# Filling tiles set around the first attention's compressed scores, a lighter first and last phase, and the second attention's maxima ahead of due evictions

## The reference

```python
# first block: compressed branch, with 31 blocks of keys and values
kc = compress(kv[0], ...); vc = compress(kv[1], ...)
pc = masked_softmax(q @ kc.T, cmp_end <= t)
o_c = pc @ vc
...            # selected and window branches: causal softmax over 512 keys
o = gates[0] * o_c + gates[1] * o_s + gates[2] * o_w
c = silu(layernorm(causal_dwconv(c_val * sigmoid(c_gate))))   # 31 taps
h = h + (sigmoid(za) * (o @ w_o) + sigmoid(zb) * (c @ w_co + b)) @ w_out
# second module, first block: 16 heads
s = q @ k.T + c[:, None] - c[None, :]      # c: running sum of log forget gates
m = softmax(causal(s)) @ v @ w_out
```

## Time and profile before

| | us |
|---|---|
| timed executions | 2183.87, 2184.62, 2186.61 |
| profiled execution, its time | 2185.68 |
| its span | 2183.9 |
| TensorE busy | 2146.1 |
| VectorE busy | 1013.6 |
| GpSimd busy | 933.8 |
| ScalarE busy | 869.6 |

### The profile page before, as it was taken

The page is one execution under the profiler, slowest core; times in us unless marked ns, Lnnn a source line. Parts: engine busy times, 40 slices in busy tenths (PEclk is TensorE's granted clock), DMA queues, the critical chain, the costliest instruction groups (busy, mean ns, idle before and its releaser), DMA issues.

```text
span 2183.9 us, 25305 instructions
## 1 busy us (share of the span) xinstructions
PE 2146.1 (98%) x10192; PEld 1758.8 (81%) x10192; DVE 1013.6 (46%) x1637; ACT 869.6 (40%) x1358; POOL 933.8 (43%) x424
## 2 busy tenths in 40 slices
PE   9999999999999999999999999999999999999998
PEld 7877778888888887777778888888888888888886
DVE  5877775445524235666634422313653345122134
ACT  5434346444424254444434422324532244233234
POOL 5722124434444455322225444444554454444446
PEclk9999999999999999999999999999999999999999
DMA  4421112233233332211122333322223323332222
GB/s 159 148 75 41 47 49 80 94 97 106 97 97 97 97 115 78 70 57 49 49 67 88 97 97 97 97 97 87 97 87 97 97 85 99 97 97 96 97 80 85
DMA packets 53829, 193.27 MB, mean 88 GB/s; under 512 B 6096, under 2 KB 6224, under 8 KB 53712
## 3 DMA queue, kind: packets, MB, share of 16 engines
q1 hardware_dynamic: 52992, 189.81, 27.0%
q10 hardware_dynamic: 720, 1.84, 0.3%
HBM read 189.53 MB, written 2.10 MB: 88 GB/s over the span
## 4 chain that ended last, share of the span: by engine, by line
PE 89%; DVE 6%; ACT 3%; issue 1%; DMA 0%; POOL 0%; DVEq 0%; ACTq 0%; POOLq 0%
PE ps L519 27%; PE ps L521 27%; PE ps L520 27%; PE ps L733 1%; DVE ps L1209 1%; PE ps L982 1%; PE ps L713 1%; PE ps L1000 1%; PE ps L725 1%; ACT w_hi L1855 1%; PE ps L615 1%; DVE xg_lo L1169 1%; PE ps L1007 0%; DVE ps L1730 0%; PE ps L715 0%
## 5 line engine op out<-in xcount | busy, mean ns | idle before, releaser
L472 POOL TENSOR_TENSOR w_lo<-w_raw,w_hi 128x1024 fp32r<-128x1024 f32 x352 | 852.6, 2424 | 1211.4 <-ACT w_hi L1855 1211.3
L519 PE MATMUL ps<-xg_hi,w_hi 128*128 128x512 f32 x1688 | 674.1, 399 | 5.4 <-POOL w_lo L486 2.8
L521 PE MATMUL ps<-xg_hi,w_lo 128*128 128x512 f32 x1688 | 661.2, 392 | 0.0
L520 PE MATMUL ps<-xg_lo,w_hi 128*128 128x512 f32 x1688 | 660.7, 391 | 0.0
L1855 ACT ACTIVATE w_hi<-w_raw 128x1024 fp32r<-128x1024 f32 x352 | 372.3, 1058 | 626.5 <-PE ps L521 623.8
L519 PEld LDWEIGHTS ps<-xg_hi,w_hi 128*128 128x128 f32 x1688 | 318.8, 189 | 69.3 <-issue 3.0
L521 PEld LDWEIGHTS ps<-xg_hi,w_lo 128*128 128x128 f32 x1688 | 318.5, 189 | 67.9
L520 PEld LDWEIGHTS ps<-xg_lo,w_hi 128*128 128x128 f32 x1688 | 319.2, 189 | 59.4
L521 PE MATMUL ps<-h_hi,w_lo 128*128 128x512 f32 x688 | 267.8, 389 | 0.0
L519 PE MATMUL ps<-h_hi,w_hi 128*128 128x512 f32 x688 | 267.8, 389 | 0.0
L520 PE MATMUL ps<-h_lo,w_hi 128*128 128x512 f32 x688 | 267.8, 389 | 0.0
(11 more groups left out here) (342 smaller groups left out, 2462.7 us busy)
## 6 DMA issues: line engine op xcount, KB each, us to landing
w_raw<-in_weights SPq DMA_DIRECT2D x352, 512.0 KB, 3.5
out_x<-mixed SPq DMA_DIRECT2D x8, 256.0 KB, 2.1
resid<-in_x SPq DMA_DIRECT2D x3, 512.0 KB, 7.4
p_raw<-in_p ACTq DMA_DIRECT2D x3, 512.0 KB, 3.6
resid<-in_x SPq DMA_DIRECT2D x2, 256.0 KB, 4.0
last_gain<-in_last_gain SPq DMA_DIRECT2D x1, 512.0 KB, 4.6
w_raw<-in_weights SPq DMA_DIRECT2D x1, 256.0 KB, 4.0
w_raw<-in_weights ACTq DMA_DIRECT2D x1, 256.0 KB, 4.4
```

What stands on the lines that cost most here:

```text
L472: pool.tensor_tensor(w_lo[:, slot, :], w_raw[:, u % RAW, :], w_hi[:, slot, :].bitcast(F32), ALU.subtract).then_inc(w_ready, 1)
L519: pe.matmul(o, w, x, start=start, stop=False)
L520: pe.matmul(o, w, xl, start=False, stop=False)
L521: return pe.matmul(o, wl, x, start=False, stop=stop)
```

## The change

In the first attention, three triples stand before `cmp_scores(0)` and one inside it, one inside each of the three later `cmp_scores`; phase 8 has nine triples in its steps where it had sixteen (the eight after the steps stay), and phases 1 to 7 keep theirs. The low parts of the compressed keys and values are made from PSUM without copies in SBUF. Two taps more stand before the phases, and the first tap of each step of phase 0 is gone, so the last taps move to the last step of phase 7. The eviction steps shift with the table (in phases 1 to 7 from steps 0 and 2 mostly to 1 and 3). In the second attention, VectorE's and ScalarE's due evictions go behind the next maxima and exponentials, the last low part of a pair goes behind the first maxima of the next pair, and the forget row of the next pair is made by ScalarE. Six matmuls that nobody reads stand before the last part of the output projection.

```diff
-EARLY_TAPS = 62
+EARLY_TAPS = 64
-LN_ADD = ((0, 1), (4, 0), (7, 3))
-NSA_FILL = [((2, 2),) * 4] + [((2, 2),) * 4, ((2, 2, 2), (2, 1), (2, 2), (2, 1))] * 4
+LN_ADD = ((2, 2), (4, 0), (7, 3))
+NSA_FILL = [((6, 2), (2, 2), (2, 2), (2, 2))] + [((2, 2), (2, 2), (2, 2), (2, 2, 1)), ((2, 2, 2), (2, 1), (2, 2), (2, 1))] * 3 + [
+    ((2, 2), (2, 2), (2, 2), (2, 2, 0)), ((2, 1, 1), (1, 1), (1, 1), (1, 0))]
...
-            def cmp_scores(p):
+            def cmp_scores(p, between):
...
+                    if qi < QB - 1 and between[qi]:
+                        fill(between[qi])
...
+            fill(3)
             pe.wait_ge(c_act, 5)
...
-            pe.wait_ge(s_cmp["klo"], 2)
+            pe.wait_ge(s_cmp["klo"], 4)
...
-                            cmp_scores(0)
-                            fill(pieces[0])
+                            cmp_scores(0, (0, 1, 0))
+                            fill(2)
...
-                        cmp_scores(j // 2 + 1)
+                        cmp_scores(j // 2 + 1, (0, pieces[2], 0))
...
             for p in range(8):
                 fox_pair(p)
+            for _ in range(6):
+                pe.matmul(ps[:, 2, :], ident_r[:], ident_r[:].unsqueeze(1).to_broadcast([P, QB, P]), start=True, stop=True)
...
-            dve.tensor_copy(kc_f[0:HD, 0:NC1], ps[0:HD, 4, 0:NC1]).then_inc(s_cmp["out"], 1)
-            dve.tensor_copy(kc_f[HD:P, 0:NC1], ps[HD:P, 4, NC1:2 * NC1]).then_inc(s_cmp["out"], 1)
-            dve.tensor_tensor(vc_f[:], ps[0:2 * NC1, 5, 0:P], own[:], ALU.mult).then_inc(s_cmp["out"], 1)
+            dve.tensor_tensor(ps[0:2 * NC1, 5, 0:P], ps[0:2 * NC1, 5, 0:P], own[:], ALU.mult).then_inc(s_cmp["out"], 1)
...
-            low(kc_lo[:], kc_f[:], kc_hi[:], s_cmp["klo"])
-            low(vc_lo[:], vc_f[:], vc_hi[:], s_cmp["klo"])
+            for g in range(2):
+                rows = slice(g * HD, (g + 1) * HD)
+                low(kc_lo[rows, 0:NC1], ps[rows, 4, g * NC1:(g + 1) * NC1], kc_hi[rows, 0:NC1], s_cmp["klo"])
...
+            dve.tensor_tensor(vc_lo[:], ps[0:2 * NC1, 5, 0:P], vc_hi[:].bitcast(F32), ALU.subtract).then_inc(s_cmp["klo"], 2)
...
-                    if tapped[0] < CT * CONV_TAPS:
+                    if j and tapped[0] < CT * CONV_TAPS:
                         taps(1)
...
-                mx(0); nrm(0); evict(0)
-                mx(1); nrm(1)
+                mx(0)
+                if p:
+                    fox_evict(p - 1, 11)
+                    out_low(p - 1, 1)
+                nrm(0)
+                mx(1); evict(0); nrm(1)
...
-                evict(1)
-                mx(2); nrm(2); evict(2)
-                mx(3); nrm(3)
-                if p < 7:
-                    head_rows(p + 1)
+                mx(2); evict(1); nrm(2)
+                mx(3); evict(2); nrm(3)
...
-                ex(0); evict(0); ex(1)
+                ex(0); ex(1); evict(0)
...
-                evict(1); ex(2); evict(2); ex(3); evict(3)
+                ex(2); evict(1); ex(3)
+                if p < 7:
+                    act.activation(c_head[:], c_rows[:], ACT.Copy, scale=head_sel[:, p + 1:p + 2]).then_inc(A2["crow"], 1)
+                evict(2); evict(3)
```

More of the change, by code:

```diff
@@ L827, in _ @@
                     if j % 2 and i == QB - 1 and j < 7:
-                        cmp_scores(j // 2 + 1)
+                        cmp_scores(j // 2 + 1, (0, pieces[2], 0))
+                    elif j == 7 and i == QB - 1:
+                        fill(pieces[2])
                     fill(pieces[1])
@@ L1263, in _ @@
                 dve.tensor_tensor(kv_dup[HD:P, j, 0:S - 1], ps[HD:P, BANK[uu], 1:S], R[HD:P, 0, 1:S], ALU.mult).then_inc(bank_free, 1)
-            dve.memset(kc_f[:], 0.0).then_inc(s_cmp["out"], 1)
+            for t in (kc_hi, kc_lo):
+                dve.tensor_scalar(t[:, NC1:NCP], ones[:, 0:1], 0.0, None, ALU.mult).then_inc(s_cmp["out"], 1)
             dve.wait_ge(s_cmp["dup"], 4)
@@ L1305, in _ @@
             dve.wait_ge(unit_done, U["cmp_out"] + 1)
[L1306 to L1309 removed]
+            dve.tensor_tensor(ps[0:2 * NC1, 5, 0:P], ps[0:2 * NC1, 5, 0:P], own[:], ALU.mult).then_inc(s_cmp["out"], 1)
             dve.memset(token[:, 12:13], 0.0).then_inc(bank_free, 1)
             dve.wait_ge(s_cmp["khi"], 2)
[L1312 to L1314 removed]
+            for g in range(2):
+                rows = slice(g * HD, (g + 1) * HD)
+                low(kc_lo[rows, 0:NC1], ps[rows, 4, g * NC1:(g + 1) * NC1], kc_hi[rows, 0:NC1], s_cmp["klo"])
+            dve.wait_ge(s_cmp["khi"], 3)
+            dve.tensor_tensor(vc_lo[:], ps[0:2 * NC1, 5, 0:P], vc_hi[:].bitcast(F32), ALU.subtract).then_inc(s_cmp["klo"], 2)
             dve.wait_ge(s_kv["lo"], 2)
@@ L1437, in _ @@
                     nsa_evict(nsa_made(j, i - 1) if i else nsa_made(j - 1, QB - 1) if j else 0)
-                    if tapped[0] < CT * CONV_TAPS:
+                    if j and tapped[0] < CT * CONV_TAPS:
                         taps(1)
-                    if i == 1 and br == 0 and j < 8:
+                    if i == (1 if j else QB - 1) and br == 0 and j < 8:
                         cmp_normalise(p)
@@ L1648, in _ @@
             dve.wait_ge(s_fg["dve"], 6)
-            def head_rows(p):
-                dve.tensor_scalar(c_head[:], c_rows[:], head_sel[:, p:p + 1], None, ALU.mult).then_inc(A2["crow"], 1)
-            head_rows(0)
+            dve.tensor_scalar(c_head[:], c_rows[:], head_sel[:, 0:1], None, ALU.mult).then_inc(A2["crow"], 1)
             counted = [3, 3]
@@ L1682, in lo, with out_low @@
                     split_turned(A2, e0 + 4 * hd + kb, kb % 2, (fpt_hi, fpt_lo), kb)
-                def out_low(hd):
+                def out_low(p, hd):
                     rows = slice(hd * HD, (hd + 1) * HD)
@@ L1690, in evict @@
                     fox_evict(p, i)
-                mx(0); nrm(0); evict(0)
-                mx(1); nrm(1)
+                mx(0)
[4 more added lines that the diff above has]
+                mx(1); evict(0); nrm(1)
                 dve.wait_ge(A2["vhi"], p + 1)
                 low(fv_lo[:], ps[:, 4, :].rearrange("p (a b) -> p a b", b=P), fv_hi[:], A2["vlo"])
-                evict(1)
-                mx(2); nrm(2); evict(2)
-                mx(3); nrm(3)
-                if p < 7:
-                    head_rows(p + 1)
+                mx(2); evict(1); nrm(2)
+                mx(3); evict(2); nrm(3)
                 evict(3)
-                lo(0, 0); lo(0, 1); evict(4); lo(0, 2); evict(5); lo(0, 3); evict(6); lo(1, 0); out_low(0); lo(1, 1); evict(7)
-                lo(1, 2); evict(8); lo(1, 3); evict(9); evict(10); out_low(1); evict(11)
+                lo(0, 0); lo(0, 1); evict(4); lo(0, 2); evict(5); lo(0, 3); evict(6); lo(1, 0); out_low(p, 0); lo(1, 1); evict(7)
+                lo(1, 2); evict(8); lo(1, 3); evict(9); evict(10)
+                if p == 7:
+                    out_low(7, 1)
             while counted[0] < 5:
@@ L1981, in _ @@
             highs(U["cmp_out"] + 1 + RING)
-            act.wait_ge(s_cmp["out"], 4)
-            copy_hi(kc_hi[:], kc_f[:], s_cmp["khi"])
-            copy_hi(vc_hi[:], vc_f[:], s_cmp["khi"])
+            act.wait_ge(unit_done, U["cmp_out"] + 1)
+            for g in range(2):
+                rows = slice(g * HD, (g + 1) * HD)
+                copy_hi(kc_hi[rows, 0:NC1], ps[rows, 4, g * NC1:(g + 1) * NC1], s_cmp["khi"])
+            act.wait_ge(s_cmp["out"], 3)
+            copy_hi(vc_hi[:], ps[0:2 * NC1, 5, 0:P], s_cmp["khi"])
             highs(U["gates"] + 1 + RING)
```

4 lines of the change are left out of this document (removed).

## The result

The changed kernel took 2193.22 us (median of 6 runs, 2191.39 to 2195.42); the kernel before, on the same chip, 2186.05 us (6 runs, 2183.87 to 2188.07). The ratio is 1.0036, with a 95% interval of 1.0025 to 1.0046: slower by 7 to 8 us, where 2175.6 was predicted. The profiled execution took 2192.44 us, with a span of 2190.7.

What follows compares the result with a forecast made beforehand. TensorE, busy 98% of the span, was taken as the bound, losing time to waits and the 1.2 GHz clock. Terms -5.8 - 1.0 + 0.3 - 1.3 - 1.3 = -9.1 us gave 2175.6 us, range 2170.8 to 2181.3.

Steps and rivals of the forecast that it cites:

- The opening: Start of the first attention: the 4.06 us wait and 4.5 of low clock go, four triples cost 2.76: -5.8 us.
- rival B: The opening still waits, klo 2 us late and the clock low again: 4.5 us come back, 2180.1 us; chance 0.06.
- The later compressed scores: Three later compressed scores, one triple inside each: +2.07 us, two low-clock episodes go, -3.1: -1.0 us.
- Evictions of phases 1 to 7 moved: Evictions go from steps 0 and 2 to 1 and 3: 0 us, bounded by 0.3 for each of seven phases.
- Phase 8: Seven triples leave, but the dependency chain sets the length; ScalarE's queue ends 0.55 earlier, ln_sum costs +0.85: +0.3 us.
- Second attention: Evictions behind maxima and forget rows on ScalarE cut waits, with some new ones in pairs 2, 5 and 7: -1.3 us.
- Unread matmuls: Six matmuls before the output projection's last part fit a 1.41 us wait and keep the clock up: -1.3 us.
- A: The clock falls anyway: two or three low-clock episodes of 1.54 us come back, 2179.4 us; chance 0.17.
- D: Slower than before: phase 8 starved, TensorE at 1.2 GHz for all of it, costing 10.3 us: 2185.8 us; chance 0.04.

Runs made afterwards that it cites:

- run 10: The kernel before with only the opening's new low parts of compressed keys and values, made from PSUM without SBUF copies: 2177.29 us, ratio 0.9961.
- run 4: The changed kernel with the filling table, taps and normalising steps of the kernel before, and eight unread matmuls for the opening's three triples: 2175.13 us, ratio 0.9956.
- run 7: run 4 without the eight unread matmuls in the opening: 2174.85 us, ratio 0.9949.
- run 12: run 7 with the eviction of fv moved ahead of the maxima again in the last pair alone: 2173.54 us, ratio 0.9946.
- run 13: The changed kernel with GpSimd's four colliding w_lo waiting until VectorE's prob_s of the step is done, in phases 0, 2, 4 and 6: 2183.22 us, ratio 0.9998.
- run 1: The changed kernel with VectorE's normalising of the compressed scores moved off the eviction steps in phases 0, 2, 4 and 6: 2183.79 us, ratio 0.9992.
- padded: The changed kernel with 21 unread matmuls in phase 8 where the seven removed filling triples had stood: 2190.07 us, ratio 1.0022.
- run 14: run 13 with one wait more: GpSimd's w_lo of phase 7's last step waits for the last ln_sum: 2180.38 us, ratio 0.9990.
- run 3: The kernel before with the second attention's part of the change alone, without the six unread matmuls: 2184.13 us, ratio 0.9998.

## Why the prediction was wrong

- **The opening, -5.8: right.** No wait before the first compressed scores and full clock behind; the subtractions from PSUM take 0.41 us for two and 0.28 beside a running `w_lo`. The second scores of phase 0, the mark that was named, start at 132.60 instead of 138.47, 5.9 us earlier. One bound was added up wrongly: with 2 us of waiting and the low clock both back, the term would be -5.8 + 2 + 4.5 = +0.7 and not -1.3, and rival B 2182.1 and not 2180.1, above the stated range; neither came, so it changes nothing here. Not seen: the three triples were not needed. Without them and the two taps the wait is 0.21 us and the whole opening gives 8.5 (run 10).
- **The later compressed scores, -1.0: wrong in size.** The triples cost their 2.07. Of the two low stretches there the one at 268 went and the other stayed, at 168: +0.5 where -1.0 was forecast. Run 10, whose later filling is that of the kernel before, has neither in its trace, and runs 4, 7 and 12 with the same filling have one near 260 (6.8, 3.4 and 3.4 us long): these stretches were no fixed cost of this place, and the -3.1 for them was not sure to be had.
- **Evictions of phases 1 to 7 moved, 0 with a bound of 0.3 each: the step that failed.** It priced VectorE's eviction at 0.7 and `w_hi` at 1.06 us and stopped there. It did not follow `w_hi` to the engine that waits for it, GpSimd's `w_lo`, nor ask what VectorE does in those 2.4 us. Measured: 5.7 us of waits in phases 2, 4 and 6, 1.3 in phase 0, and clock with them; 8.3 us by run 13. The prediction had the rule in hand: it names the exclusive port pair of the Trainium skill's page SBUF — State Buffer, "Who interferes with whom", for the opening, and used it for what leaves the shared port but not for what is moved under it. The same section of the Trainium skill also says that `tensor_scalar` can take both ports when its operands allow it, and that a two-input instruction from SBUF contends for the shared one. The traces agree on these forms: the stretched `prob_s` is of the first kind, `prob_c` and `ln_sum` of the second, and `pt_lo<-ps,pt_hi`, with one operand in PSUM, was never stretched beside `w_lo` (0.68 or 0.69 us for 128x512 in every case).
- **Phase 8, +0.3: the chain was read rightly.** From the turn of step 0 to the values of step 3 it takes 16.76 us, where it took 16.81. From the mean to the mix it is 27.0 us with any filling (27.08 before, 26.99 in run 1, 27.04 padded), plus 1.6 in the changed kernel for one low stretch, the upper bound that was named. The waits for `pt_lo` in it sum to 4.2 us where some 5 were forecast. `ln_sum` was mis-sized: 1.72 instead of 0.85, since it collides with `w_lo` too (0.76 without, run 14). What was not drawn out is the consequence: if the chain sets the length, every triple moved out of it is paid again elsewhere. It was booked, 2.76 and 2.07, but inside terms that looked like gains. All terms of the new table but the evictions sum to +2.1 in the forecast (2.76 - 1.0 + 0.3), and runs 7 and 14 show +9.0. Of these 7 us too little, up to 3.1 is the clock counted as a gain, which run 10's trace has without any triple inside the scores, and some 1.4 is the stage's own length (6.5 against 5.1 without clock effects); the rest no run takes apart.
- **Second attention, -1.3: right in kind, -0.4 measured** (run 3). Pair 5's 1.30 went; the `fv` wait it forecast as +0.45 was +0.65, and the waits of pairs 0 and 1 fell by 0.4 and 0.2, not by 0.9.
- **Unread matmuls, -1.3: right for their place, nothing in the changed kernel's sum.** The wait of 1.41 and the low stretch at 1114 are gone; the six fill it exactly:

```profile
1121.56 1.60 PE L1039 MATMUL ps<-ident_r 128*128 128x512 f32 x6
1123.13 0.50 PE L518 MATMUL ps<-fo_hi,w_hi 128*128 128x512 f32 x1
```

  But one low stretch stands 18 us earlier now, behind the wait for `fv`:

```profile
1096.74 0.47 PE L518 MATMUL ps<-fo_hi,w_hi 128*128 128x512 f32 x1 [1.16 <-DVE fv L1149]
```
```profile
1097.00:1101.00 4.00, 4.00 (x19) 2.80 (x19) 1.81 (x6) 0.00 (x0) 1.16 (x1) 0.57 0.45 126
```

  Runs 3 and 7 have the same wait of 1.16 and no low clock behind it, so this stretch is not that wait's alone. In run 7 the unread matmuls left no low stretch in or behind the second attention, and there the term held.

- **Rivals.** None was the one that came. A (the clock falls anyway) came in part, three stretches in the first attention; D had the sign but not the mechanism: phase 8 was not at 1.2 GHz throughout. The range was too sure of the term of 0: its bound came from the moved instructions' own durations.
